# The first gather and the first expert of a fused decoder layer: samples turned instead of gathered, waits by halves, the token weights' turn moved

## What is computed

```
logits = xt @ w_router + b_router             # 264 tokens x 32 experts, 4 experts per token
for e in range(32):
    a = xt @ w_gate_up[e] + b_gate_up[e]      # 1024 -> 2 x 1024
    gate = minimum(a[:, :1024], 7); up = clip(a[:, 1024:], -7, 7)
    h = (up + 1) * gate * sigmoid(1.702 * gate)
    out = out + combine[:, e] * (h @ w_down[e] + b_down[e])
```

## Time and profile before

| | |
|---|---|
| median of 3 runs | 1426.2 us (1424.7 to 1426.3) |
| the profiled execution | 1424.4 us, its span 1422.5 us |
| PE busy | 1343.6 us (94%) |
| DVE, ACT, POOL busy | 353.2, 252.7, 83.9 us |
| mean DMA rate over the span | 348 GB/s |
| chain that ended last | PE 76%, DMA 20%, DVE 3% |
| mean granted clock of TensorE | 0.986 of full speed |

### The profile page before, as it was taken

One profiled execution on the slowest core, in us unless ns is written; L12 is line 12 of the kernel. 1 busy time (PEld: TensorE's weight loads), 2 busy tenths in 40 slices (PEclk: granted clock), 3 DMA queues, 4 the chain that ended last, 5 costly groups with the idle time before them and its releaser, 6 DMA issues.

```text
span 1422.5 us, 17783 instructions
## 1 busy us (share of the span) xinstructions
PE 1343.6 (94%) x7308; PEld 718.1 (50%) x7308; DVE 353.2 (25%) x775; ACT 252.7 (18%) x541; POOL 83.9 (6%) x104
## 2 busy tenths in 40 slices
PE   7999999999999989999999889899999998998987
PEld 5757887588887734434434334344344243342422
DVE  2762442310234522212201112112122121220112
ACT  3423331511123401111101011011111010110102
POOL 1550212000101000000000000000000000000000
PEclk9999999999999999999999999999999999999999
DMA  9783465833737799999999999999999999999995
GB/s 329 241 313 113 154 207 146 312 119 119 281 133 296 303 379 391 425 428 428 429 428 429 429 428 428 428 428 428 420 428 429 428 430 428 428 428 428 428 428 237
DMA packets 62437, 494.75 MB, mean 348 GB/s; under 512 B 5247, under 2 KB 6472, under 8 KB 37816
## 3 DMA queue, kind: packets, MB, share of 16 engines
q1 hardware_dynamic: 50904, 453.95, 77.1%
q0 software_dynamic: 11488, 40.17, 8.4%
HBM read 487.05 MB, written 7.05 MB: 347 GB/s over the span
## 4 chain that ended last, share of the span: by engine, by line
PE 76%; DMA 20%; DVE 3%; issue 1%; SPq 0%; ACT 0%; POOL 0%; DVEq 0%
PE bank L1183 21%; PE bank L680 16%; PE bank L1210 13%; DMA ring<-in_w_gate_up 11%; DMA arena<-in_w_down 8%; PE bank L1169 4%; PE bank L1222 4%; PE bank L639 3%; PE bank L652 2%; PE bank L1190 1%; PE bank L704 1%; PE bank L790 1%; PE bank L1196 1%; PE bank L1119 1%; PE bank L1033 1%
## 5 line engine op out<-in xcount | busy, mean ns | idle before, releaser
L1183 PE MATMUL bank<-ring,arena 128*64 128x512 f32 x1536 | 345.9, 599 | 8.0 <-DMA ring<-in_w_gate_up 7.3
L1210 PE MATMUL bank<-arena 128*64 128x512 f32 x976 | 223.8, 609 | 30.7 <-DMA arena<-in_w_down 30.7
L1183 PEld LDWEIGHTS bank<-ring,arena 128*64 128x64 f32 x1536 | 105.2, 137 | 227.1 <-issue 209.1
L680 PE MATMUL bank<-arena,ring 128*128 128x264 f32 x896 | 204.9, 388 | 0.0
L680 PEld LDWEIGHTS bank<-arena,ring 128*128 128x128 f32 x896 | 168.2, 190 | 31.9 <-issue 3.9
L1210 PEld LDWEIGHTS bank<-arena 128*64 128x64 f32 x976 | 68.8, 140 | 171.7 <-issue 126.5
L2208 DVE TENSOR_TENSOR resid<-resid,bank 128x264 f32<-128x264 f32 x128 | 54.9, 429 | 375.0 <-PE bank L1222 373.5
L1183 PE MATMUL bank<-arena 128*64 128x512 f32 x512 | 115.5, 593 | 3.3 <-DMA arena<-in_w_gate_up 3.3
L2213 DVE TENSOR_SCALAR arena<-bank 128x512 f32<-128x512 f32 x32 | 22.0, 687 | 318.5 <-PE bank L1183 318.5
L1660 ACT COPY arena<-bank 64x512 f32<-64x512 f32 x63 | 36.5, 580 | 237.9 <-PE bank L1210 237.1
L1183 PEld LDWEIGHTS bank<-arena 128*64 128x64 f32 x512 | 36.6, 137 | 77.5 <-issue 67.4
(11 more groups left out here) (314 smaller groups left out, 975.0 us busy)
## 6 DMA issues: line engine op xcount, KB each, us to landing
ring<-in_w_gate_up SPq DMA_DIRECT2D x96, 2048.0 KB, 28.9
arena<-in_w_down SPq DMA_DIRECT2D x61, 2048.0 KB, 22.2
arena<-in_w_gate_up SPq DMA_DIRECT2D x32, 2048.0 KB, 28.8
ring<-in_w_in SPq DMA_DIRECT2D x10, 2048.0 KB, 10.9
ring<-in_w_down SPq DMA_DIRECT2D x3, 2048.0 KB, 44.6
out<-arena POOLq DMA_DIRECT2D x10, 512.0 KB, 5.3
arena<-in_state_gla POOLq DMA_DIRECT2D x8, 512.0 KB, 4.8
ring<-in_w_o_mla SPq DMA_DIRECT2D x2, 2048.0 KB, 8.5
```

What stands on the lines that cost most here:

```text
L680: mm = nc.tensor.matmul(lin_bank(name)[0:m, 0:width], w(ring_name, nk, cols)[:, k, a:a + m], rhs[:, k, 0:width], start=(k == 0), stop=(k = ...
L1183: mm = nc.tensor.matmul(B[i // 2][CAP * (i % 2):CAP * (i % 2) + CAP, :], xg[:, k, CAP * e:CAP * e + CAP], slot(n)[:, a:a + 512], start=Fal ...
L1210: mm = nc.tensor.matmul(B[4][CAP * half:CAP * half + CAP, :], hT[:, c, CAP * (k // 4):CAP * (k // 4) + CAP], slot(j)[:, a:a + 512], start= ...
```

## The change

1. The first gather (`gather(0)`, `gather(1)`) takes two tiles, as the later ones do. Between its halves stand eight transposes of 8 rows (8 tokens x 128 values, `hn_tok[0:8, 2, ...]`) into free columns of bank 4. ScalarE copies them into the samples' seats of both experts, after the first half's columns; the second half's columns follow.
2. PE waits for the first half (`x_pair` 2m + 1, and the samples' copies, `rows_copied` 7) before the first four chunks of gate-up, and for the second half before the last four. In later pairs this wait is split in the same way.
3. `cwt` is turned between the fourth and the fifth chunk of expert 0, no longer after the eighth.

```diff
-            def gather(half, tiles=2):
+            def gather(half):
                 for k in range(4):
                     a = P * (k + 4 * half)
-                    for tt, (_, n) in enumerate(TILES[:tiles]):
-                        mm = nc.tensor.matmul(B[2 + 3 * half][:, P * k:P * k + P], hn_tok[0:n, tt, a:a + P], sel[0:n, tt, :], start=(tt == 0), stop=(tt == tiles - 1))
+                    for tt in range(2):
+                        mm = nc.tensor.matmul(B[2 + 3 * half][:, P * k:P * k + P], hn_tok[:, tt, a:a + P], sel[:, tt, :], start=(tt == 0), stop=(tt == 1))
                 mm.then_inc(S("gathered"), 1)
...
-                pe.wait_ge(S("x_pair"), 2 * m + 2)
+                pe.wait_ge(S("x_pair"), 2 * m + 1)
+                if first and isinstance(m, int):
+
+                    pe.wait_ge(S("rows_copied"), 7)
                 gate_up_rows(0, 4, 0, p, q)
                 if not first:
                     turn_hidden(n - 1)
-                gate_up_rows(4, KC, 0, p, q)
                 if first and isinstance(m, int):
                     pe.wait_ge(S("routed"), 1)
                     turn("cwt", [(t0, cw[0:n, tt, 0:32]) for tt, (t0, n) in enumerate(TILES)])
+                pe.wait_ge(S("x_pair"), 2 * m + 2)
+                gate_up_rows(4, KC, 0, p, q)
...
-            gather(0, 3)
-            gather(1, 3)
+            gather(0)
+            for k in range(KC):
+                mm = nc.tensor.transpose(B[4][:, 64 + SAMPLE * k:64 + SAMPLE * k + SAMPLE], hn_tok[0:SAMPLE, 2, P * k:P * k + P], ident[0:SAMPLE, 0:SAMPLE])
+            mm.then_inc(S("rows_turned"), 1)
+            gather(1)
...
-                places = CAP if isinstance(g, int) and g == 0 else SEATS
                 for half in range(2):
                     act.wait_ge(S("gathered"), 2 * g + half + 1)
-                    nc.scalar.copy(xg[:, 4 * half:4 * half + 4, :].rearrange("p k (e c) -> p k e c", e=2)[:, :, :, 0:places],
-                                   B[2 + 3 * half][:].rearrange("p (k e c) -> p k e c", k=4, e=2)[:, :, :, 0:places]).then_inc(S("x_pair"), 1)
+                    nc.scalar.copy(xg[:, 4 * half:4 * half + 4, :].rearrange("p k (e c) -> p k e c", e=2)[:, :, :, 0:SEATS],
+                                   B[2 + 3 * half][:].rearrange("p (k e c) -> p k e c", k=4, e=2)[:, :, :, 0:SEATS]).then_inc(S("x_pair"), 1)
+                    if half == 0 and isinstance(g, int) and g == 0:
+
+                        act.wait_ge(S("rows_turned"), 7)
+                        for e in range(2):
+                            ins = nc.scalar.copy(xg.rearrange("p k (e c) -> p k e c", e=2)[:, :, e, SEATS:CAP],
+                                                 B[4][:, 64:64 + SAMPLE * KC].rearrange("p (k s) -> p k s", k=KC))
+                        ins.then_inc(S("rows_copied"), 1)
```

## The result

| | before | with the change |
|---|---|---|
| median of 6 runs | 1426.5 us (1424.7 to 1430.4) | 1419.6 us (1418.5 to 1421.9) |
| profiled execution | 1424.4 us, span 1422.5 | 1419.8 us, span 1418.0 |

The ratio is 0.9949, with a 95% interval of 0.9939 to 0.9959: 7.3 us faster, between 5.8 and 8.7. The forecast was 1418.8 us. The measured median is 0.8 us above it and inside the range.

The account below looks back on a forecast made before the run. The weight stream was taken as the bound, with PE late only in one short stretch. Gaps of 1.97, 2.20, 0.67 and 2.54 us, together 7.4, would close: 1426.2 - 7.4 = 1418.8 us, range 1416.0 to 1422.3.

Parts of the forecast that it names:

- The bound: Weight stream to the end: four stretches from 503 to 547 us lose 7.4 us, and the gain is what they return.
- a rival's 6.7: If an 8-row matmul costs no more than a full one, the down issue comes 6.7 us earlier: 1419.5 us; shared chance 0.15.
- The gather: First gather without its 8-row tile: -4.68 us of matmuls, turns added; PE starts gate-up 4.1 us earlier (0.7 to 4.5).
- The term for the eight turns: Eight 8-row transposes inside the first gather: 0.92 us plus 0.35 us for changes of rows, 1.27 us.
- The rule on the load of weights: PE's weight load takes time by columns, not rows; by it 1419.5 us, doubted for alternating rows; shared chance 0.15.
- 0.35 us for two changes: First gather: part of an 8-row matmul's 0.585 us, charged to switching between 128 and 8 rows.
- VectorE's work and the clips: Before expert 1's bias: VectorE's 2.8 us hidden under gate-up, PE goes on 6.8 us earlier after 1.6 us of idleness.
- The clock: At expert 1's bias and gate-up: no fall expected after 1.6 us of idleness, saving 0.89 + 1.43 = 2.3 us.
- The sum: PE reaches the first down product 9.1 us earlier, more than the stream can take; gain 7.4 us, 1418.8 us.
- The leads: Load issues at three gaps come 3.6, 6.1 and 3.4 us before the queue is empty; 1.2 to 1.7 needed.
- The rivals: Small tiles cheap or half works, chance 0.15; gain lost at 999 us, 0.10; slower through clock falls, 0.05.
- come back at 999 us: Where SP's two loops meet, the stream would wait for PE to free a slot: no gain, 1426.2 us; chance 0.10.

Follow-up runs that it names:

- The block of small rows: Kernel before with its first gather reordered, in each half eight 128-row matmuls, then four 8-row ones: -2.4 us (-3.7 to -1.3) against before.
- The delay of 10.5 us: Changed kernel with 96 identity transposes, result unused, on PE between the first gather and first gate-up: +1.3 us (0.0 to +2.7) against the kernel before.

## Why the prediction was right

Point by point, in its own order.

- **The bound.** Right. The gain is the stream's, though the measured time by itself (5.8 to 8.7 us) cannot tell 7.4 us from a rival's 6.7. The traces show whose gain it is: in the eleven profiles of kernels that keep SP's loads as they are, the time to the last gate-up piece less what the stream lost is 877.4 us, within 0.8 us, whichever way PE's lead was changed.
- **The gather.** The term for the eight turns was too high: 1.27 us forecast, 0.59 to 0.73 measured (4.46 - 3.73), also below the 0.9 to 1.7 us that it named as a sign. It took 0.115 us for a turn from records that use all 128 rows; the turns followed each other by 0.062 us. PE started 4.67 us earlier, not 4.1. It changed nothing, since the lead was spare.
- **The rule on the load of weights.** The forecast gave it 1419.5 us as a rival, and the median of 1419.6 cannot tell that from 1418.8. PE's start of gate-up can: 1.7 us earlier by the rule, 4.67 measured. So for alternating rows the rule by itself does not give the cost. The block of small rows settles it: an 8-row matmul by itself costs what a full one costs, 0.112 us a record. What the forecast called 0.35 us for two changes measured 0.38. The Trainium skill, TensorE: Matmul & The Clock Gate, section on what happens when you issue a matmul, says of the load of weights that its time does not depend on the number of rows. The trace agrees inside a block, and the cost of the changes comes on top.
- **VectorE's work and the clips.** Right: idleness 1.48 us against 1.6 forecast, cover of 4.08 us.
- **The clock.** Right that it would stay up. Its price was set at 2.3 us from the rows before; with the fall in other places it was 2.95 us on PE.
- **The sum.** 9.1 us of lead at the down load forecast, 9.6 measured; 7.4 us of gaps, of which 7.2 went. The median fell by 7.0 us. That this is so close is in part luck: from the gather to the end of the span the two profiles of the change are 6.4 and 6.6 us shorter than the one before (925.3 and 925.1 against 931.7).
- **The leads.** 3.4 us at the down load forecast, of which 1.2 to 1.7 are needed: 1.7 to 2.2 us to spare. The delay of 10.5 us measured 2.0 to 2.3.
- **The rivals.** The gain did not come back at 999 us: the seam lost 0.8 us against 0.7. The clock fell nowhere between 962 us and the last 3 us.

The profiled execution gained only 4.5 us in its span. 1.9 us of the missing is the later start of the gather. The rest, 884.2 - 878.0 = 6.2 against 7.2 us of gaps, stays open: over 820 us, a tenth of a per cent of the stream's rate is 0.8 us, and the rows show whole GB/s.

## What to carry to other kernels

When a queue of transfers is full almost everywhere, look for the few places where it runs dry, work out each one's loss from the bytes, and ask which release came late: a saving on the compute engine counts up to that sum and not beyond. Give each idle stretch its full price, the lateness and the restart of the empty queue, here 0.5 to 1.0 and 1.2 to 1.7 us. And a small serial piece of work on a third engine can be moved under a product that needs nothing of it: VectorE's 2.8 us and the clock's 2.3 to 2.95 us came from moving three transposes.

## What was not expected

- Changing between matmuls of 128 and of 8 rows cost 0.19 us each time, more than a record of a small matmul (0.112 us).
- With 16 more instructions in PE's program, PE stood 0.9 and 1.75 us near the end for nothing that the profile shows, while 96 more, or 36 in another place, did nothing of the kind. Where the instructions lie may matter; that is a guess, and nothing here tested it.
- The start of the first gather varied from 487.3 to 494.3 us between the profiles of kernels that change nothing ahead of it. The two shown first differ in both directions: the change's is 0.8 us ahead at its products near 40 us (39.78 against 40.54), 4.4 us behind where PE resumes at 112.04 against 107.66, and 1.9 us behind at the gather, although of the two only the kernel before had a fall of the clock at 257 us. This is as large as the gain, and it is why medians of five runs say less here than a trace read from a fixed instruction on.
